# Last gate stage of a decoder layer: embedding products first, woven with the first gate tile

## The chip, the cores and the metric

The kernel runs on one core of a Trainium2 chip. Its time is that of one execution on the device, in microseconds (us). Three runs of the kernel before took 2184.57, 2187.47 and 2188.53 us; the median, 2187.47, is the time before.

## The reference

One layer of a decoder is computed for 1024 prompt positions and 8 single positions of other requests, together 1032 tokens (`N`), with 1024 channels. All of its stages lie ahead of the one that is changed, which is the end of the layer:

```python
    f = (jax.nn.silu(h2 @ w_ffn_gate) * (h2 @ w_ffn_up)) @ w_ffn_down
    x = x + rms_norm(f, ln_ffn_post)
    e = ple @ w_ple
    x = x + rms_norm(jax.nn.sigmoid(x @ w_ple_gate) * e, ln_ple_post)
```

`ple` is a per-layer input of 256 channels per token (`p_prompt`, `p_sample`), `w_ple` is 256 x 1024, `w_ple_gate` 1024 x 1024. The products `e` need `ple` alone; the gate needs the updated `x`.

## The kernel before, in words

The kernel is one program in stages, each with a barrier of all engines at its end. Within a stage every engine has its own list of instructions in the order in which the code issues them, and semaphores (`wait_ge`, `then_inc`) are all that sets the order between engines. Activations lie with channels on the 128 partitions and tokens along them: `X` is 8 chunks of 128 channels by 1032 tokens. A result tile is 128 output channels by 1032 tokens and takes three banks of PSUM (344 columns each); `acc` in PSUM has two such areas.

To keep fp32 accuracy at the speed of the faster matmul type, gate products are split: weights W = hi + lo (`WS`, parts 0 and 1), activations = hi + lo (`HH` and `XL`), and `split_tile` (L573) issues hi x HH, hi x XL, lo x HH, three matmuls each, for each of 8 chunks: 72 matmuls per tile. GpSimd splits the weights, with a cast (L581) and a subtraction (L583). The embedding products are plain fp32, in `gemm_tile` (L560): 2 chunks x 3 matmuls, each of which shows as two records.

The stage `ple` (L2370 on) does this:

- Entry. TensorE sums the squares of `f` per token (`row_sums`, L518); VectorE and ScalarE make the root's inverse (`RowRoot`, L546 to L553); TensorE spreads it over 128 partitions (`row_spread`, L526) into the second area of `acc`, called `flat`. SyncE has loaded the embedding input into `ptok`; TensorE transposes it (L2415, L2417) into `tp`, from where ScalarE copies it to `pT` (L2447).
- Update of X, chunk by chunk (c = 0 to 7): VectorE scales f by the gain and `flat` (L2467), adds it to X (L2470); ScalarE rounds X to `HH` (L2449); VectorE forms the remainder `XL` (L2473).
- Eight tiles m, as loops (`Fori`) on each engine. TensorE: 72 gate matmuls into area 0, then six embedding matmuls into area 1. ScalarE: sigmoid of area 0 to `SA` (L2453). VectorE: `SA` times area 1, into `F` chunk m (L2478). Then the square (ScalarE, L357), its sum (VectorE, L363) and the gain (ScalarE, L2457). Weights: SyncE loads the gate tile's into slot 0 of `W` and the embedding tile's into slot 1; GpSimd splits slot 0 into slot 0 of `WS` once `gate_done` says that TensorE is done with the tile before.

The first gate tile waits chunk by chunk for `XL` (`wait=(pe, x_lo)`). The stage after, `store_y`, adds the last norm and writes the output.

Of the kernel before, what the change touches and what calls it, by code (L numbers as in the profile page):

```python
# [508 lines left out]
def weight(ap, at, cols=P):  # L509

    return ap[:, bass.ds(at, cols)].rearrange("(c p) m -> p c m", p=P)
# [1858 lines left out]
def ple(k):  # L2370

    nc, g = k.nc, k.g
    with Stage(k, "ple") as st:
        acc = st.psum("acc", [P, 2, NT, 512])
        tp = st.psum("tp", [P, 2, 512])
        p_in, tr_done, tr_copied, gate_done, e_done, sig, gated, hi_done, split_done, slot_ok, spread, mixed, x_new, x_hi, x_lo, scaled = st.sems(
            "p_in tr_done tr_copied gate_done e_done sig gated hi_done split_done slot_ok spread mixed x_new x_hi x_lo scaled")
        ptok = k.E[:, 0:9 * 256].rearrange("p (t f) -> p t f", f=256)
        pT = chunks(k.Z[:, 8 * N:10 * N], 2)
        SA = k.E[:, 0:N]  # L2380
        squares = SquareSum(k, st)
        root = RowRoot(k, st, "post")
        flat = acc[:, 1].rearrange("p n w -> p (n w)")[:, 0:N]
        base = list(k.wcount)
        for s in range(2):
            k.wcount[s] += 8 * 16
        block = st.block()

        @block.sync
        def _(sp):  # L2390
            sp.dma_start(ptok[:, 0:TT, :], g["p_prompt"].rearrange("(t p) f -> p t f", p=P)).then_inc(p_in, 16)
            sp.dma_start(ptok[0:B, TT, :], g["p_sample"]).then_inc(p_in, 16)
            with sp.Fori(0, 8) as m:

                sp.wait_ge(split_done, m + 1)
                sp.dma_start(k.W[:, 0, 0:8, :], weight(g["w_ple_gate"], m * P)).then_inc(k.wfull[0], 16)
                sp.wait_ge(e_done, m + 1)
                sp.dma_start(k.W[:, 1, 0:2, :], weight(g["w_ple"], m * P)).then_inc(k.wfull[1], 16)

        @block.tensor  # L2400
        def _(pe):
            pe.sem_inc(gate_done, 1)
            pe.sem_inc(e_done, 1)
# [3 lines left out]
            pe.wait_ge(p_in, 32)  # L2407
            for c in range(2):
                for q in range(3):
                    n = 3 * c + q  # L2410
                    if n >= 2:
                        pe.wait_ge(tr_copied, n - 1)
                    if q < 2:
                        for t in range(4):
                            last = nc.tensor.transpose(tp[:, n % 2, t * P:(t + 1) * P], ptok[:, 4 * q + t, c * P:(c + 1) * P], k.ident[:])  # L2415
                    else:
                        last = nc.tensor.transpose(tp[:, n % 2, 0:B], ptok[0:B, TT, c * P:(c + 1) * P], k.ident[0:B, 0:B])  # L2417
                    last.then_inc(tr_done, 1)
            pe.wait_ge(tr_copied, 6)
            with pe.Fori(0, 8) as m:  # L2420
                pe.wait_ge(split_done, m + 2)
                pe.wait_ge(sig, m + 1)
                split_tile(k, acc, 0, 0, k.HH, k.XL, DC, wait=(pe, x_lo)).then_inc(gate_done, 1)
                pe.wait_ge(mixed, DC)
                pe.wait_ge(k.wfull[1], 16 * m + base[1] + 16)
                pe.wait_ge(gated, m + 1)
                gemm_tile(k, acc, 1, pT, 2).then_inc(e_done, 1)

        @block.gpsimd
        def _(pool):  # L2430
            pool.sem_inc(split_done, 1)
            with pool.Fori(0, 8) as m:
                pool.wait_ge(k.wfull[0], 16 * m + base[0] + 16)
                pool.wait_ge(gate_done, m + 1)
                pool.sem_inc(slot_ok, 1)
                split_weights(k, pool, 0, 0, DC, hi_done, m, split_done)

        @block.scalar
        def _(act):
            act.sem_inc(sig, 1)  # L2440
            root.scalar(act)
            for c in range(DC):
                if c < 6:
                    f, q = c // 3, c % 3
                    act.wait_ge(tr_done, c + 1)
                    a, w = (q * 512, 512) if q < 2 else (T, B)
                    nc.scalar.activation(pT[:, f, a:a + w], tp[:, c % 2, 0:w], ACT.Copy).then_inc(tr_copied, 1)  # L2447
                act.wait_ge(x_new, c + 1)
                nc.scalar.activation(k.HH[:, c, :], k.X[:, c, :], ACT.Copy).then_inc(x_hi, 1)  # L2449
            with act.Fori(0, 8) as m:  # L2450
                act.wait_ge(gate_done, m + 2)
                act.wait_ge(gated, m + 1)
                nc.scalar.activation(tokens(SA), acc[:, 0, :, 0:NW], ACT.Sigmoid).then_inc(sig, 1)  # L2453
                act.wait_ge(gated, m + 2)
                squares.square(act, one(k.F, m), m, 0)
                act.wait_ge(squares.squared, m + 1)
                nc.scalar.activation(one(k.F, m), one(k.F, m), ACT.Copy, scale=k.gains[:, 4, bass.ds(m, 1)]).then_inc(scaled, 1)  # L2457

        @block.vector
        def _(dve):  # L2460
            dve.sem_inc(gated, 1)
            root.clear(dve)
            root.vector(dve, acc[:, 0, 0, 0:9])
            dve.wait_ge(spread, 1)
            for c in range(DC + 1):
                if c < DC:
                    nc.vector.scalar_tensor_tensor(out=k.F[:, c, :], in0=k.F[:, c, :], scalar=k.gains[:, 3, c:c + 1], in1=flat,  # L2467
                                                   op0=ALU.mult, op1=ALU.mult).then_inc(mixed, 1)
# [6 lines left out]
            with dve.Fori(0, 8) as m:  # L2475
                dve.wait_ge(sig, m + 2)
                dve.wait_ge(e_done, m + 2)
                nc.vector.tensor_tensor(one(k.F, m), tokens(SA), acc[:, 1, :, 0:NW], ALU.mult).then_inc(gated, 1)  # L2478
                squares.add(dve, m, 0)
            dve.wait_ge(gated, 9)  # L2480
            dve.wait_ge(squares.summed, DC + 2)


# [144 lines left out]
```

## Time and profile before

| | us |
|---|---|
| runs | 2184.57, 2187.47, 2188.53; median 2187.47 |
| profiled execution, its own time | 2183.83 |
| its span, first to last instruction | 2182.1 |
| last gate stage, first matmul to end of its last sum | 1995.6 to 2151.9 |
| TensorE busy in the span | 2039.9 (93%) |
| VectorE, GpSimd, ScalarE busy | 754.3, 614.6, 507.6 |
| mean granted TensorE clock | 0.961 |

Over the whole span TensorE is the busy engine, but the change touches 7% of the span, so the shares of the whole say little here: read the stage's own stretches. Names of a tile in a row are those of its memory: `Z` holds `F`, `pT` and `XL`, `E` holds `ptok`, `SA` and the squares, `ple_acc` and `ple_tp` are the stage's PSUM. PE is TensorE's matmuls, PEld its weight loads, DVE VectorE, ACT ScalarE, POOL GpSimd, SPq the DMAs that SyncE issues.

### The profile page before, as it was taken

How to read it: one execution, taken by the hardware profiler on the slowest of the kernel's cores; microseconds unless marked ns; L12 is line 12 of the kernel's file. 1: busy time of each engine (PE TensorE's matmuls, PEld its weight loads, DVE VectorE, ACT ScalarE, POOL GpSimd, SP SyncE). 2: the span in 40 equal slices, each digit the busy share in tenths (PEclk: the TensorE clock that was granted, in tenths of full speed). 3: DMA queues.
4: the chain of work that ended last, by engine and by line, in shares of the span. 5: the costliest groups of instructions: out<-in, count | busy, mean ns of one | idle time of the engine just before them, and what ended most of it. 6: DMA issues, size and time to landing. Idle time of an engine off the chain costs nothing. (4 is left out here: it accounts for less than half of the span.)

```text
span 2182.1 us, 33339 instructions
## 1 busy us (share of the span) xinstructions
PE 2039.9 (93%) x13732; PEld 1944.9 (89%) x13732; DVE 754.3 (35%) x1440; ACT 507.6 (23%) x920; POOL 614.6 (28%) x506
## 2 busy tenths in 40 slices
PE   7999999976799989999989899999999999997897
PEld 6999989854688879999989899999999999996886
DVE  4104433233778863122231523012212322334413
ACT  5121011123577771010022311110000000012323
POOL 2323200001445553233332123232233323321110
PEclk9999999977899999999999799999999999998999
DMA  6233354133100011111122311111112112113012
GB/s 236 60 107 106 89 215 155 39 134 158 55 2 2 2 55 44 53 35 53 30 58 105 110 39 43 44 49 48 41 46 58 35 42 58 45 37 125 27 45 81
DMA packets 159027, 150.82 MB, mean 69 GB/s; under 512 B 18712, under 2 KB 151394, under 8 KB 156034
## 3 DMA queue, kind: packets, MB, share of 16 engines
q1 hardware_dynamic: 156082, 111.43, 16.7%
q0 software_dynamic: 2304, 33.56, 3.9%
q10 hardware_dynamic: 528, 4.23, 0.5%
q8 instruction: 83, 1.36, 0.3%
q14 instruction: 30, 0.25, 0.0%
HBM read 132.28 MB, written 21.10 MB: 70 GB/s over the span
## 5 line engine op out<-in xcount | busy, mean ns | idle before, releaser
L573 PE MATMUL ffn_acc<-HH,WS 128*128 128x344 f32 x2112 | 395.8, 322 | 8.4 <-DVE HL L505 7.3
L581 POOL CAST WS<-W 128x1024 fp32r<-128x1024 f32 (+2 forms) x125 | 130.9, 1047 | 901.2 <-PE ffn_acc L573 542.5
L573 PEld LDWEIGHTS ffn_acc<-HH,WS 128*128 128x128 f32 x2112 | 345.0, 189 | 8.8 <-issue 7.3
L583 POOL TENSOR_TENSOR WS<-W,WS 128x1024 fp32r<-128x1024 f32 (+2 forms) x125 | 294.7, 2357 | 10.0
L573 PE MATMUL ffn_acc<-HL,WS 128*128 128x344 f32 x1056 | 225.3, 322 | 0.0
L573 PE MATMUL ffn_acc<-AH,WS 128*128 128x344 f32 x1056 | 195.4, 320 | 0.0
L573 PEld LDWEIGHTS ffn_acc<-HL,WS 128*128 128x128 f32 x1056 | 179.9, 190 | 0.0
L573 PE MATMUL proj_acc<-HH,WS 128*128 128x344 f32 x912 | 174.4, 324 | 5.7 <-DVE HL L505 5.7
L573 PEld LDWEIGHTS ffn_acc<-AH,WS 128*128 128x128 f32 x1056 | 171.7, 188 | 0.0
L573 PEld LDWEIGHTS proj_acc<-HH,WS 128*128 128x128 f32 x912 | 149.0, 189 | 6.6 <-issue 4.1
L573 PE MATMUL merge_acc<-HH,WS 128*128 128x344 f32 x768 | 146.7, 323 | 7.0 <-DVE HL L505 7.0
L573 PEld LDWEIGHTS merge_acc<-HH,WS 128*128 128x128 f32 x768 | 126.8, 190 | 7.4 <-issue 5.6
L1029 PE MATMUL cmp_pre<-Hr,CW 128*128 128x254 f32 (+1 forms) x576 | 121.7, 371 | 2.7 <-DMA CW<-in_cmp_w_k 2.7
L1029 PEld LDWEIGHTS cmp_pre<-Hr,CW 128*128 128x128 f32 x576 | 105.0, 194 | 14.5 <-DMA CW<-in_cmp_w_k 2.9
L573 PE MATMUL ffn_acc<-AL,WS 128*128 128x344 f32 x528 | 111.7, 320 | 0.0
L1833 POOL TENSOR_SCALAR Hr<-Hr,tiny,gtok 128x128 f32<-128x128 f32 (+7 forms) x129 | 84.2, 661 | 93.4 <-DVE tiny L1913 63.3
L2343 DVE TENSOR_TENSOR E<-ffn_acc,R 128x1032 f32<-128x1032 f32 x22 | 27.1, 1233 | 221.9 <-PE ffn_acc L573 216.3
L2302 ACT ACTIVATE E<-E 128x1032 f32<-128x1032 f32 x22 | 23.5, 1068 | 334.8 <-DVE E L2343 334.8
L573 PE MATMUL proj_acc<-HL,WS 128*128 128x344 f32 x456 | 96.9, 321 | 0.0
L573 PEld LDWEIGHTS ffn_acc<-AL,WS 128*128 128x128 f32 x528 | 88.5, 188 | 0.0
L573 PE MATMUL ple_acc<-HH,WS 128*128 128x344 f32 x384 | 74.2, 325 | 10.2 <-ACT Z L2447 6.9
L573 PE MATMUL merge_acc<-HL,WS 128*128 128x344 f32 x384 | 82.3, 323 | 0.0
(408 smaller groups left out, 3325.5 us busy)
## 6 DMA issues: line engine op xcount, KB each, us to landing
W<-in_w_in SPq DMA_DIRECT2D x30, 512.0 KB, 3.9
W<-in_w_ffn_gate SPq DMA_DIRECT2D x22, 512.0 KB, 3.8
W<-in_w_ffn_up SPq DMA_DIRECT2D x22, 512.0 KB, 3.9
W<-in_w_ffn_down SPq DMA_DIRECT2D x16, 384.0 KB, 3.3
W<-in_w_ffn_down SPq DMA_DIRECT2D x16, 320.0 KB, 3.0
kept_x<-Z SPq DMA_DIRECT2D x1, 4128.0 KB, 13.4
Z<-kept_x SPq DMA_DIRECT2D x1, 4128.0 KB, 14.4
kept_x<-Z ACTq DMA_DIRECT2D x1, 4128.0 KB, 11.6
```

The lines of the kernel that those rows point to most:

```text
L573: last = k.nc.tensor.matmul(acc[:, s, n, 0:NW], k.WS[:, ws, part, c, :], src[:, c, n * NW:(n + 1) * NW], start=(c == 0 and part == 0 and s ...
L581: k.nc.gpsimd.tensor_copy(k.WS[:, ws, 0, 0:nk, :], w).then_inc(hi_done, 1)
L583: k.nc.gpsimd.tensor_tensor(k.WS[:, ws, 1, 0:nk, :], w, k.WS[:, ws, 0, 0:nk, :].bitcast(F32), ALU.subtract).then_inc(split_done, 1)
L1029: last = nc.tensor.matmul(pre[:, i, 0:2 * n].rearrange("p (g n) -> p g n", g=2), w1[:, i, c, :], TR[:, i, c % 8, :, c // 8:c // 8 + n], st ...
L1833: nc.gpsimd.tensor_scalar(x, x, li[s % 2][:, j:j + 1], k.gtok[:, t, 3 * h + r:3 * h + r + 1], ALU.mult, ALU.mult).then_inc(p_ready, 1)
L2302: nc.scalar.activation(SL, SL, ACT.Silu).then_inc(silu_done, 1)
L2343: nc.vector.tensor_tensor(tokens(SL), acc[:, 0, :, 0:NW], tokens(k.R1[:]), ALU.mult).then_inc(scaled, 1)
```

## The change

The stage is written straight out, without loops on the engines, and in another order.

- All of `w_ple` is loaded at once, into its own place `we`, ahead of the gate weights; these then take both slots of `W` and of `WS` in turn, and the first two loads wait for nothing.
- Eight of the transposes stand ahead of the row spread. The spread is copied to SBUF (`R1`) by ScalarE, and VectorE's scaling reads it there.
- The embedding product of chunk c goes into area 1 and is copied by ScalarE into `F` chunk c, whose old content has been used by then. On TensorE the products alternate with the chunks of gate tile 0: E0, E1, gate chunk 0, E2, gate chunk 1, and so on to gate chunk 7.
- Gate tiles 1 to 7 follow, in the two areas in turn. `SA` has two halves. VectorE multiplies `SA` by `F` chunk m, both in SBUF.

```diff
-            k.wcount[s] += 8 * 16
+            k.wcount[s] += 4 * 16
...
+            sp.dma_start(we, g["w_ple"].rearrange("(c p) m -> p c m", p=P)).then_inc(e_in, 16)
+            for m in range(8):
+                if m >= 2:
+                    sp.wait_ge(split_done, m - 1)
+                sp.dma_start(k.W[:, m % 2, 0:8, :], weight(g["w_ple_gate"], m * P)).then_inc(k.wfull[m % 2], 16)
...
             row_sums(k, acc[:, 0, 0, 0:9], k.ssq).then_inc(root.mean, 1)
+            pe.wait_ge(p_in, 32)
+            for n in range(2):
+                for t in range(4):
+                    last = nc.tensor.transpose(tp[:, n, t * P:(t + 1) * P], ptok[:, 4 * n + t, 0:P], k.ident[:])
+                last.then_inc(tr_done, 1)
             pe.wait_ge(root.rooted, 1)
             row_spread(k, flat, root.rs).then_inc(spread, 1)
...
-            with pe.Fori(0, 8) as m:
-                pe.wait_ge(split_done, m + 2)
-                pe.wait_ge(sig, m + 1)
-                split_tile(k, acc, 0, 0, k.HH, k.XL, DC, wait=(pe, x_lo)).then_inc(gate_done, 1)
-                pe.wait_ge(mixed, DC)
-                pe.wait_ge(k.wfull[1], 16 * m + base[1] + 16)
-                pe.wait_ge(gated, m + 1)
-                gemm_tile(k, acc, 1, pT, 2).then_inc(e_done, 1)
+            pe.wait_ge(r_copied, 1)
+            pe.wait_ge(e_in, 16)
+            for c in range(DC + 1):
+                if c < DC:
+                    if c:
+                        pe.wait_ge(e_copied, c)
+                    for i in range(2):
+                        for n in range(NT):
+                            last = nc.tensor.matmul(acc[:, 1, n, 0:NW], we[:, i, c * P:(c + 1) * P], pT[:, i, n * NW:(n + 1) * NW],
+                                                    start=(i == 0), stop=(i == 1))
+                    last.then_inc(e_done, 1)
+                if c:
+                    if c == 1:
+                        pe.wait_ge(split_done, 1)
+                        pe.wait_ge(root.inverse, 2)
+                    pe.wait_ge(x_lo, c)
+                    last = split_tile(k, acc, 0, 0, k.HH, k.XL, c, first=c - 1, more=c < DC)
+            last.then_inc(gate_done, 1)
+            for m in range(1, 8):
+                pe.wait_ge(split_done, m + 1)
+                if m == 1:
+                    pe.wait_ge(e_copied, DC)
+                else:
+                    pe.wait_ge(sig, m - 1)
+                split_tile(k, acc, m % 2, m % 2, k.HH, k.XL, DC).then_inc(gate_done, 1)
...
+            for m in range(8):
+                pool.wait_ge(k.wfull[m % 2], base[m % 2] + 16 * (m // 2 + 1))
+                if m >= 2:
+                    pool.wait_ge(gate_done, m - 1)
+                split_weights(k, pool, m % 2, m % 2, DC, hi_done, m, split_done)
...
             root.scalar(act)
+            turned(0)
+            turned(1)
+            act.wait_ge(spread, 1)
+            nc.scalar.activation(k.R1[:], flat, ACT.Copy).then_inc(r_copied, 1)
+            for n in range(2, 6):
+                turned(n)
             for c in range(DC):
                 act.wait_ge(x_new, c + 1)
                 nc.scalar.activation(k.HH[:, c, :], k.X[:, c, :], ACT.Copy).then_inc(x_hi, 1)
+                act.wait_ge(e_done, c + 1)
+                nc.scalar.activation(tokens(k.F[:, c, :]), acc[:, 1, :, 0:NW], ACT.Copy).then_inc(e_copied, 1)
+            for m in range(8):
+                act.wait_ge(gate_done, m + 1)
+                if m >= 2:
+                    act.wait_ge(gated, m - 1)
+                nc.scalar.activation(tokens(SA[:, m % 2, :]), acc[:, m % 2, :, 0:NW], ACT.Sigmoid).then_inc(sig, 1)
...
-            dve.wait_ge(spread, 1)
+            dve.wait_ge(r_copied, 1)
...
+                nc.vector.tensor_tensor(k.F[:, m, :], SA[:, m % 2, :], k.F[:, m, :], ALU.mult).then_inc(gated, 1)
```

On TensorE, at the stage's entry, behind the row sums (rows with - are of before, with + of after):

```order
 L518 MATMUL ple_acc<-ones,E 8x1
+L2406 MATMUL ple_tp<-ident,E 128x128 x8
 L526 MATMUL ple_acc<-ident,tiny 128x128 x8
 L526 MATMUL ple_acc<-ident,tiny 128x8
+L2418 MATMUL ple_tp<-ident,E 128x8
 L2415 MATMUL ple_tp<-ident,E 128x128 x8
-L2417 MATMUL ple_tp<-ident,E 128x8
-L2415 MATMUL ple_tp<-ident,E 128x128 x8
-L2417 MATMUL ple_tp<-ident,E 128x8
```

Half of the big transposes now stand ahead of the spread (L526).

On TensorE of before, the end of a tile in the loop:

```order
L573 MATMUL ple_acc<-XL,WS 128x344 x3
L573 MATMUL ple_acc<-HH,WS 128x344 x3
L2425 ISA
L560 MATMUL ple_acc<-Z,W 128x344 x6
L2420 REGISTER_ALU
L2420 COMPARE_AND_BRANCH
```

and of after, the beginning of the woven first tile (L2430 are the embedding products):

```order
L2430 MATMUL ple_acc<-Z 128x344 x12
L573 MATMUL ple_acc<-HH,WS 128x344 x3
L573 MATMUL ple_acc<-XL,WS 128x344 x3
L573 MATMUL ple_acc<-HH,WS 128x344 x3
L2430 MATMUL ple_acc<-Z 128x344 x6
```

The embedding products moved from behind each of the eight tiles to between the chunks of the first.

On ScalarE, what stands between the entry and the second chunk of X (HH is the rounded X, the last row the copy of an embedding product):

```order
+L2463 ACTIVATE Z<-ple_tp 128x512 x2
+L2469 ACTIVATE R<-ple_acc 128x1032
+L2463 ACTIVATE Z<-ple_tp 128x8
+L2463 ACTIVATE Z<-ple_tp 128x512 x2
+L2463 ACTIVATE Z<-ple_tp 128x8
+L2474 ACTIVATE HH<-X 128x1032
+L2476 ACTIVATE Z<-ple_acc 128x1032
```

All six copies of the transposed input now stand ahead of the first HH, and a product's copy behind each HH.

## Rows read from the trace of the kernel before

**Rows 1.** Busy us by stretch: length, PE, PEld, DVE, ACT, POOL (x instructions), clock, DMA, GB/s.
```profile
2004.50:2022.60 18.10, 4.16 (x18) 2.97 (x19) 17.91 (x15) 7.50 (x11) 2.09 (x1) 0.59 0.10 29
...
2039.90:2147.90 108.00, 105.30 (x588) 94.72 (x588) 17.15 (x14) 31.79 (x28) 20.33 (x12) 1.00 0.13 38
```
**Rows 2.** Timeline of one tile: start, duration, engine, line, instruction, idle before.
```profile
2039.96 0.46 PEld L573 LDWEIGHTS ple_acc<-HH,WS 128*128 128x128 f32 x3 [0.93 <-issue]
...
2051.24 3.24 PEld L560 LDWEIGHTS ple_acc<-Z,W 128*128 128x128 f32 x12
2051.39 3.63 PE L560 MATMUL ple_acc<-Z,W 128*128 128x344 f32 x12
...
2051.73 1.04 POOL L581 CAST WS<-W 128x1024 fp32r<-128x1024 f32 x1 [11.98 <-PE ple_acc L573]
2052.84 2.35 POOL L583 TENSOR_TENSOR WS<-W,WS 128x1024 fp32r<-128x1024 f32 x1
...
2055.44 0.71 PE L573 MATMUL ple_acc<-HH,WS 128*128 128x344 f32 x3 [0.41 <-POOL WS L583]
```
**Rows 3.** Timeline of the stage's entry and of the update of X.
```profile
1995.29 0.39 SPq L2391 DMA_DIRECT2D E<-in_p_prompt  x1
...
1995.63 3.67 PE L518 MATMUL ple_acc<-ones,E 128*128 128x1 f32 x18 [5.08 <-PEq L90]
...
2000.18 4.30 PE L526 MATMUL ple_acc<-ident,tiny 128*128 128x128 f32 x18 [0.88 <-ACT tiny L553]
...
2004.52 1.29 DVE L2467 SCALAR_TENSOR_TENSOR Z<-Z,gains,ple_acc 128x1032 f32<-128x1032 f32 x1 [4.64 <-PE ple_acc L526]
2005.54 0.60 ACT L2447 ACTIVATE Z<-ple_tp 128x512 f32<-128x512 f32 x1 [5.41 <-PE ple_tp L2415]
2005.85 1.83 DVE L2470 TENSOR_TENSOR X<-X,Z 128x1032 f32<-128x1032 f32 x1
...
2009.31 1.12 PE L2415 MATMUL ple_tp<-ident,E 128*128 128x128 f32 x4 [2.90 <-ACT Z L2447]
...
2022.60 1.20 PE L573 MATMUL ple_acc<-HH,WS 128*128 128x344 f32 x3 [6.95 <-ACT Z L2447]
...
2029.27 1.28 DVE L2467 SCALAR_TENSOR_TENSOR Z<-Z,gains,ple_acc 128x1032 f32<-128x1032 f32 x1
```
**Rows 4.** Short stretches of the entry and of the first tile (columns of rows 1).
```profile
1996.50:2000.00 3.50, 2.80 (x15) 2.69 (x15) 0.43 (x3) 0.23 (x2) 0.00 (x0) 0.50 0.90 292
...
2022.60:2025.80 3.20, 3.20 (x11) 3.20 (x12) 3.17 (x4) 1.07 (x1) 0.00 (x0) 0.50 0.00 0
...
2005.00:2005.50 0.50, 0.50 (x5) 0.50 (x4) 0.50 (x1) 0.00 (x0) 0.50 (x1) 0.66 0.00 0
```
**Rows 5.** The gate weights' loads: issue to landing.
```profile
DMA to landing us min/median/max: 3.9/4.0/6.3
```
**Rows 6.** Timeline of the projection stage: gate-type (L573) and fp32 (L754) matmuls.
```profile
244.20 0.64 PE L573 MATMUL proj_acc<-HH,WS 128*128 128x344 f32 x3
244.68 3.73 PE L754 MATMUL proj_acc<-Z,E 128*128 128x128 f32 x32
248.17 0.71 PE L573 MATMUL proj_acc<-HH,WS 128*128 128x344 f32 x3
```
**Rows 7.** Timeline of the stage's end.
```profile
2143.74 0.64 PE L573 MATMUL ple_acc<-HH,WS 128*128 128x344 f32 x3
...
2144.48 1.28 ACT L2453 ACT_TABLE_LOAD   x1 [8.08 <-PE ple_acc L573]
2145.78 1.03 ACT L2453 ACTIVATE E<-ple_acc 128x1032 f32<-128x1032 f32 x1
2148.08 1.23 DVE L2478 TENSOR_TENSOR Z<-E,ple_acc 128x1032 f32 x1 [11.71 <-PE ple_acc L560]
...
2150.63 1.23 DVE L363 TENSOR_TENSOR E<-E 128x1032 f32<-128x1032 f32 x1 [1.33 <-ACT E L357]
```
**Rows 8.** The same add in the stage before: duration ns min/median/max.
```profile
L2331 DVE TENSOR_TENSOR Z<-Z x8: 1232/1232/2420, 1205.3 to 1233.6; 128x1032 f32<-128x1032 f32 x8
```

More of the change, by code:

```diff
@@ L2405, in _ @@
             pe.wait_ge(root.rooted, 1)
             row_spread(k, flat, root.rs).then_inc(spread, 1)
[L2407 to L2418, printed above, removed]
@@ L2419, in _ @@
-            pe.wait_ge(tr_copied, 6)
-            with pe.Fori(0, 8) as m:
-                pe.wait_ge(split_done, m + 2)
-                pe.wait_ge(sig, m + 1)
-                split_tile(k, acc, 0, 0, k.HH, k.XL, DC, wait=(pe, x_lo)).then_inc(gate_done, 1)
-                pe.wait_ge(mixed, DC)
-                pe.wait_ge(k.wfull[1], 16 * m + base[1] + 16)
-                pe.wait_ge(gated, m + 1)
-                gemm_tile(k, acc, 1, pT, 2).then_inc(e_done, 1)
+            for n in range(2, 6):
+                q = n % 3
+                pe.wait_ge(tr_copied, n - 1)
+                if q < 2:
+                    for t in range(4):
+                        last = nc.tensor.transpose(tp[:, n % 2, t * P:(t + 1) * P], ptok[:, 4 * q + t, P:2 * P], k.ident[:])
+                else:
+                    c = n // 3
+                    last = nc.tensor.transpose(tp[:, n % 2, 0:B], ptok[0:B, TT, c * P:(c + 1) * P], k.ident[0:B, 0:B])
+                last.then_inc(tr_done, 1)
@@ L2438, in _, with turned @@
         @block.scalar
         def _(act):
-            act.sem_inc(sig, 1)
-            root.scalar(act)
-            for c in range(DC):
[L2443 to L2447, printed above, removed]
+            def turned(n):
+                f, q = n // 3, n % 3
+                act.wait_ge(tr_done, n + 1)
+                a, w = (q * 512, 512) if q < 2 else (T, B)
+                nc.scalar.activation(pT[:, f, a:a + w], tp[:, n % 2, 0:w], ACT.Copy).then_inc(tr_copied, 1)
@@ L2448, in _ @@
+            root.scalar(act)
+            turned(0)
+            turned(1)
+            act.wait_ge(spread, 1)
+            nc.scalar.activation(k.R1[:], flat, ACT.Copy).then_inc(r_copied, 1)
+            for n in range(2, 6):
+                turned(n)
+            for c in range(DC):
                 act.wait_ge(x_new, c + 1)
                 nc.scalar.activation(k.HH[:, c, :], k.X[:, c, :], ACT.Copy).then_inc(x_hi, 1)
-            with act.Fori(0, 8) as m:
-                act.wait_ge(gate_done, m + 2)
+                act.wait_ge(e_done, c + 1)
+                nc.scalar.activation(tokens(k.F[:, c, :]), acc[:, 1, :, 0:NW], ACT.Copy).then_inc(e_copied, 1)
@@ L2465, in _ @@
             for c in range(DC + 1):
                 if c < DC:
[L2467 removed]
+                    nc.vector.scalar_tensor_tensor(out=k.F[:, c, :], in0=k.F[:, c, :], scalar=k.gains[:, 3, c:c + 1], in1=k.R1[:],
                                                    op0=ALU.mult, op1=ALU.mult).then_inc(mixed, 1)
@@ L2474, in _ @@
             squares.start(dve)
[L2475 to L2480, printed above, removed]
+            dve.wait_ge(e_copied, DC)
+            for m in range(8):
+                dve.wait_ge(sig, m + 1)
+                nc.vector.tensor_tensor(k.F[:, m, :], SA[:, m % 2, :], k.F[:, m, :], ALU.mult).then_inc(gated, 1)
+                squares.add(dve, m, m % 2)
+            dve.wait_ge(gated, 8)
             dve.wait_ge(squares.summed, DC + 2)
```

29 lines of the change are left out of this document (8 added, 21 removed).

## The prediction

> **What bounds the kernel now.** Read the stretches first: which engine works through the last gate stage, and when. From 2004.50 to 2022.60 us TensorE is busy 4.16 of 18.10 us, while VectorE updates X chunk by chunk; in the seven tiles after the first one TensorE is busy 105.30 of 108.00 us [rows 1]. So the stage has a part in which TensorE stands still and a part in which nothing else matters. The timeline of one tile gives the price of each: weight loads of the gate products begin at 2039.96 and those of the embedding products at 2051.24, so 72 gate matmuls take 11.28 us; six embedding products take 3.63 us; then TensorE waits 0.41 us for GpSimd, which can split the next weights only when the gate tile is over, since there is one buffer [rows 2]. A tile takes 108.00/7 = 15.43 us [rows 1]. ScalarE and VectorE are off this path except at the end [rows 7].
>
> The timeline of the entry shows why TensorE stands still [rows 3]: row sums end at 1999.30, the row spread runs 2000.18 to 2004.48, VectorE starts its eight chunks at 2004.52, and the transposes of the embedding input wait for ScalarE, whose copies stand between the HH copies. The gate tile begins at 2022.60 after a wait of 6.95 us on the last of those copies. Nothing in the embedding products needs X: this idle time can take them.
>
> **The change, part by part.** I place everything on the profile's clock and compare the end of the stage, 2150.63 + 1.23 = 2151.86 us before [rows 7]. What follows it (norm, transposes, stores) is unchanged and is counted at nothing.
>
> *Entry, later than before.* Eight transposes now stand between the row sums and the spread, and wait for the embedding input. It is issued at 1995.29 [rows 3] and has 1.05 MB (sizes here are the shapes' elements, four bytes each); at 292 GB/s [rows 4] from 1996.5 its bytes are there at 2000.1, and I add 0.8 (an estimate) until its semaphore is up: 2000.9. At the low clock four transposes took 1.12 us [rows 3], eight 2.2, so the spread starts at 2003.1 instead of 2000.18 and ends after 4.30 at 2007.4. Bounds: 1999.3, where TensorE is ready anyway, so 1.6 earlier; and the case that the queue mixes its transfers (rival A). VectorE now waits for ScalarE's copy of the spread to SBUF as well, 0.1 + 1.03 (the sigmoid of the same shape [rows 7]): its chain starts at 2008.5, 4.0 later. That is covered, below.
>
> *First embedding product.* After the spread: its copy 1.13, four transposes 1.12, their copy 0.10 + 0.60 [rows 3], and 0.6 (an estimate) for the 8-column pieces and hand-overs: 3.5, hence 2010.9. Its weights, 1 MB behind the embedding input, are due 1.05/0.292 = 3.6 us after it, near 2004.5; the first two gate tiles' weights 1.8 us each behind, 2006.3 and 2008.1, and their splits of 3.5 us (2051.73 to 2055.19 [rows 2]) end near 2009.8 and 2013.3. All before they are needed.
>
> *TensorE's work.* The sum of products is what it was: 8 x (11.28 + 3.63) = 119.3 us. Added waits:
> - The second product wants the area of the first, with no gate chunk between: 0.1 + 1.03 for ScalarE's copy, 1.2 in all.
> - From the third on a gate chunk, 9 x 11.28/72 = 1.41 us, stands between, against 0.1 + 1.03 + 0.05 = 1.18 for the copy: hidden. The cover is thin, so 0.5 for six, with bounds of nothing and 0.5 each.
> - Clock. The first tile of before ran 2022.60 to 2025.80 at 0.50 (1.2 GHz), then at 2.4 GHz. It had been at 2.4 GHz already from about 2005.3 on, when the spread and eight transposes had run one behind the other, and was lost again in the idle time [rows 4]. Now spread, transposes and products follow each other with gaps of about 1 us, so the first product may start at either level: nothing or 1.6 (half of 3.2); I take 0.8.
> - Waits of gate chunks for X: XL of chunk 0 is due 8 us into VectorE's chain (two rounds of 3.54, the first and last of eight starts being 2004.52 and 2029.27 [rows 3], and hand-overs), near 2016, with two splits beside it 2018.4 at worst; the chunk is wanted after the second product, at 2010.9 + 0.8 + 3.63 + 1.2 + 3.63 = 2020.2. Later, VectorE needs 3.54 per chunk and TensorE 3.63 + 1.41 = 5.04. No wait; should the cover go, it costs at most the 1 to 2 us by which XL would be late.
> - Going to and fro between the two kinds of product: in the projection, also written straight out, gate-type matmuls end at 244.84, fp32 ones start at 244.68 and the next gate-type start at 248.17 before those end at 248.41 [rows 6]. Nothing, from both sides; the same rows price straight-line code.
>
> So the last gate product ends at 2010.9 + 119.3 + 1.2 + 0.5 + 0.8 = 2132.7.
>
> *Tiles 1 to 7.* Two weight slots and two accumulators: the split (3.5 us) now lies under an 11.28 us tile, and the 0.41 wait [rows 2] goes, seven times. A sigmoid must have read an accumulator two tiles later: 11 us of cover. Next late would be ScalarE, 31.79/7 = 4.5 us busy per tile [rows 1]: far off.
>
> *Tail.* Before, the last embedding product hid the sigmoid; now sigmoid 0.10 + 1.03, then multiply, square, sum, 2151.86 - 2148.08 = 3.78 [rows 7]: with 0.05 hand-over 4.95. The table load (1.28) happens once, at the first tile, not on the path. End: 2137.7. Against 2151.86 that is 14.2 us less. The multiply now reads two SBUF operands; nothing splits weights beside the last one.
>
> Profiled execution: 2183.83 - 14.2 = 2169.6 us. It lies 3.64 below the median 2187.47 of the runs; by the median the forecast is **2173.3 us**.
>
> **Two rules weighed.** VectorE's add took 1.83 instead of 1.23 with a split beside it [rows 3], and the same kind in the stage before up to 2.42 [rows 8]. The Trainium skill (SBUF — State Buffer, "SBUF: two separate sides") says that VectorE with two SBUF inputs and GpSimd take a shared port pair by exclusive lock, and the loser stands for the whole instruction; the trace agrees. It speaks against this change, since the scaled add now takes the spread from SBUF: two splits at worst 2.4 us on VectorE's chain. By the rule the end moves only if the 1.8 to 4 us of cover named above fail.
>
> The gate weights, issued behind the embedding input, landed after 6.3 us [rows 5]. The skill (DMA: Bandwidth & Descriptors, "Queues, rings and completion order") says that each DMA engine consumes descriptors in ring order; by it the megabyte of weights now queued behind does not delay the input. No row has the input's own landing.
>
> **Rivals.**
> - A, the transfers share the queue: the embedding input lands with the last of 1.05 + 1.05 + 0.52 + 0.52 = 3.14 MB, 10.8 us after 1996.5 at 292 GB/s, at 2007.3 instead of 2000.9. Everything in the stage moves by up to 6.4: 2176 to 2179.7. For it: nothing waited on this transfer, so its landing is unseen. Against: the gate weights behind it landed within 6.3 us [rows 5], in which 292 GB/s move 1.8 MB, hardly more than these two transfers (1.57).
> - B, hand-overs: each product waits half a microsecond for its area, and a lock delays the first gate chunk: 7 x 0.5 - 0.5 + 1.5 = 4.5: 2177.8. For it: a cover of 1.41 against 1.18. Against: ScalarE starts 0.10 after a tile's end [rows 7].
> - C, the slower one: the clock. If TensorE's waits in the woven first tile keep it at 1.2 GHz, its 8 x 3.63 + 11.28 = 40.3 us take 40.3 longer: 2213. It decides from 14.2 us of work at half clock. For it: the clock stood at 0.50 at the start of the first tile. Against: it rose 3.2 us after that start, although that tile had waits too.
> - D, straight-line code: some 580 matmuls that were a loop of 78 must be fetched. 1.25 us lost per tile eats 10 us: 2183, no change. Against: the projection's straight tiles run without a gap [rows 6].
>
> **Chances and range.** Forecast 0.62, A 0.15, B 0.15, D 0.05, C 0.03. Best: input there at once (-1.6), no waits (-0.5), warm start (-0.8), and the medians' scatter of 2 to 3 us: about 2166. Worst of A and B together reaches 2184; 2182 leaves out that corner, C and most of D. Range 2166 to 2182. Faster by over 0.2% (4.4 us, about what can be told from no change): forecast, A and B, 0.92; same, D, 0.05; slower, C, 0.03.
>
> **What would show it.** First embedding product near 2011, last gate product near 2133, tiles 1 to 7 at 11.3 us with no wait on GpSimd, woven chunks at 5.0 us, one table load for eight sigmoids, transposes starting near 2001, stage end near 2138. Wrong if chunks take over 5.6, if VectorE's XL is named before a gate chunk, or if the granted clock is 0.5 after the first product.

## The result, and the profile after

The changed kernel takes 2169.32 us (median of four runs, 2163.83 to 2171.33), the kernel before 2186.78 beside it (four runs, 2184.57 to 2188.53): a ratio of 0.9912, with a 95% interval of 0.9893 to 0.9931. The forecast was 2173.3 and "faster". The profiled execution's own time is 2169.65.

Because the part of the program ahead of the stage takes a few microseconds more or less from one execution to the next, I compare lengths inside one profile: from the start of the row sums (L518) to the end of the last sum (L363). Before, this was 2151.86 - 1995.63 = 156.23 us [rows 3, 7]; after, 140.23. Measured from the issue of the embedding input it is 156.57 and 140.28: 16.3 us less, of a forecast 14.2.

The stretches first, with the columns of [rows 1]: the end of the entry, the first embedding product, the woven tile, tiles 1 to 7.

```profile
2006.80:2010.40 3.60, 2.55 (x18) 1.92 (x17) 1.40 (x1) 2.21 (x5) 3.45 (x3) 0.97 0.33 81
2010.50:2013.50 3.00, 3.00 (x5) 1.84 (x6) 2.96 (x3) 0.06 (x1) 2.92 (x2) 0.50 0.56 168
2014.00:2052.80 38.80, 37.68 (x164) 28.40 (x163) 29.00 (x23) 16.82 (x17) 1.62 (x1) 1.00 0.05 14
2052.90:2132.50 79.60, 79.59 (x505) 79.30 (x503) 22.54 (x14) 22.84 (x21) 26.39 (x12) 1.00 0.09 27
```

The 14 us in which TensorE stood still while VectorE updated X [rows 1] are gone: from 2014 on it is idle 1.1 us in all, and in the seven tiles not at all. What is new is the second line: right after a stretch at 0.97 the first product starts at 0.50, that is 1.2 GHz.

The timeline of the entry (start, duration, engine, line, instruction, idle before and what ended it):

```profile
1997.01 0.39 SPq L2392 DMA_DIRECT2D E<-in_p_prompt  x1
...
1997.06 3.67 PE L518 MATMUL ple_acc<-ones,E 128*128 128x1 f32 x18 [4.78 <-PEq L90]
...
2002.60 1.97 PE L2406 MATMUL ple_tp<-ident,E 128*128 128x128 f32 x8 [1.88 <-DMA E<-in_p_sample]
...
2004.36 3.54 PE L526 MATMUL ple_acc<-ident,tiny 128*128 128x128 f32 x18
...
2009.08 0.66 PE L2415 MATMUL ple_tp<-ident,E 128*128 128x128 f32 x4 [0.54 <-ACT Z L2463]
...
2010.49 5.38 PE L2430 MATMUL ple_acc<-Z 128*128 128x344 f32 x12 [0.60 <-ACT Z L2463]
...
2013.33 3.38 DVE L2495 SCALAR_TENSOR_TENSOR Z<-Z,gains,R 128x1032 f32<-128x1032 f32 x1
...
2017.00 3.74 PE L2430 MATMUL ple_acc<-Z 128*128 128x344 f32 x12 [1.12 <-ACT Z L2476]
2017.90 1.23 DVE L2501 TENSOR_TENSOR XL<-X,HH 128x1032 fp32r<-128x1032 f32 x1
...
2020.31 0.90 PE L573 MATMUL ple_acc<-HH,WS 128*128 128x344 f32 x3
```

The transposes wait 1.88 us for the input, the second product 1.12 for its area. VectorE's second scaling takes 3.38 instead of 1.29 [rows 3], with a weight split beside it; still the first XL is ready at 2019.13, before the first gate chunk wants it at 2020.31, which shows no wait.

Two of the woven chunks, and the end (same columns):

```profile
2040.33 1.03 ACT L2476 ACTIVATE Z<-ple_acc 128x1032 f32<-128x1032 f32 x1 [2.90 <-PE ple_acc L2430]
...
2041.56 3.63 PE L2430 MATMUL ple_acc<-Z 128*128 128x344 f32 x12
...
2045.22 1.03 ACT L2476 ACTIVATE Z<-ple_acc 128x1032 f32<-128x1032 f32 x1 [2.91 <-PE ple_acc L2430]
```

```profile
2131.85 0.64 PE L573 MATMUL ple_acc<-HH,WS 128*128 128x344 f32 x3
2132.53 1.03 ACT L2481 ACTIVATE E<-ple_acc 128x1032 f32<-128x1032 f32 x1 [6.67 <-PE ple_acc L573]
2133.59 1.23 DVE L2506 TENSOR_TENSOR Z<-E,Z 128x1032 f32<-128x1032 f32 x1 [7.66 <-ACT E L2481]
...
2136.06 1.23 DVE L363 TENSOR_TENSOR E<-E 128x1032 f32<-128x1032 f32 x1 [1.24 <-ACT E L357]
```

A woven chunk takes 4.89 us, with no wait ahead of the product. The end, from the last matmul to the last sum, is 2137.29 - 2132.49 = 4.80 us.

### The profile page after: what moved, and what is told of

It is laid out like the page before. It is cut to its first block and busy times, and to the rows that moved or that the text cites. A ratio compares the mean times of both kernels' runs of the same rounds, so it can differ in the third digit from the quotient of the medians.

```text
span 2167.8 us, 33107 instructions
## 1 busy us (share of the span) xinstructions
PE 2041.6 (94%) x13732; PEld 1949.5 (90%) x13732; DVE 762.9 (35%) x1440; ACT 507.4 (23%) x922; POOL 621.9 (29%) x506
## 3 DMA queue, kind: packets, MB, share of 16 engines
q8 instruction: 87, 1.43, 0.3%
## 5 line engine op out<-in xcount | busy, mean ns | idle before, releaser
L573 PE MATMUL ffn_acc<-HH,WS 128*128 128x344 f32 x2112 | 395.7, 322 | 8.5 <-DVE HL L505 7.4
L573 PEld LDWEIGHTS ffn_acc<-HH,WS 128*128 128x128 f32 x2112 | 345.0, 189 | 8.9 <-issue 7.5
L583 POOL TENSOR_TENSOR WS<-W,WS 128x1024 fp32r<-128x1024 f32 (+2 forms) x125 | 301.6, 2413 | 10.0
L573 PE MATMUL ffn_acc<-HL,WS 128*128 128x344 f32 x1056 | 225.2, 322 | 0.0
L573 PE MATMUL ffn_acc<-AH,WS 128*128 128x344 f32 x1056 | 195.4, 320 | 0.0
L573 PE MATMUL proj_acc<-HH,WS 128*128 128x344 f32 x912 | 174.3, 324 | 7.3 <-DVE HL L505 7.3
L573 PEld LDWEIGHTS ffn_acc<-HL,WS 128*128 128x128 f32 x1056 | 179.8, 190 | 0.0
L573 PEld LDWEIGHTS ffn_acc<-AH,WS 128*128 128x128 f32 x1056 | 171.7, 188 | 0.0
L573 PEld LDWEIGHTS proj_acc<-HH,WS 128*128 128x128 f32 x912 | 149.1, 189 | 8.0 <-issue 6.0
L573 PE MATMUL merge_acc<-HH,WS 128*128 128x344 f32 x768 | 146.8, 323 | 6.8 <-DVE HL L505 6.8
L573 PEld LDWEIGHTS merge_acc<-HH,WS 128*128 128x128 f32 x768 | 126.9, 191 | 7.3 <-issue 5.5
L573 PE MATMUL ffn_acc<-AL,WS 128*128 128x344 f32 x528 | 111.7, 319 | 0.0
L573 PE MATMUL proj_acc<-HL,WS 128*128 128x344 f32 x456 | 97.2, 322 | 0.0
L573 PEld LDWEIGHTS ffn_acc<-AL,WS 128*128 128x128 f32 x528 | 88.5, 188 | 0.0
L573 PE MATMUL merge_acc<-HL,WS 128*128 128x344 f32 x384 | 82.3, 323 | 0.0
L2350 DVE TENSOR_TENSOR E<-E,ffn_acc 128x1032 f32<-128x1032 f32 x22 | 27.1, 1230 | 151.8 <-PE ffn_acc L573 151.8
```

Of the source, the lines that this page charges most:

```text
L573: last = k.nc.tensor.matmul(acc[:, s, n, 0:NW], k.WS[:, ws, part, c, :], src[:, c, n * NW:(n + 1) * NW], start=(c == 0 and part == 0 and s ...
L583: k.nc.gpsimd.tensor_tensor(k.WS[:, ws, 1, 0:nk, :], w, k.WS[:, ws, 0, 0:nk, :].bitcast(F32), ALU.subtract).then_inc(split_done, 1)
L2350: nc.vector.tensor_tensor(tokens(GU), tokens(SL), acc[:, 1, :, 0:NW], ALU.mult).then_inc(gated, 1)
```

## The experiments

All lengths below run from the start of the row sums to the end of the last sum; a length in an "expected" text that is counted from the issue of the input is 0.05 us more (before the change 0.34). Before: 156.23; changed kernel, "after" below: 140.23, 140.38 and 140.41 in three profiles. The table sums up what each kernel's profile shows.

| kernel | stage, us | first product starts after, lasts | second product's wait |
|---|---|---|---|
| before | 156.23 | - | - |
| two slots only | 154.65 | - | - |
| changed, one weight slot | 186.85 | 13.40, 3.74 | 1.12 |
| changed, not woven | 147.16 | 13.39, 3.74 | 1.42 |
| changed, spread first | 138.79 | 13.10, 3.74 | 1.12 |
| changed | 140.23 | 13.43, 5.38 | 1.12 |
| two areas | 139.09 | 13.69, slow | none |
| weights issued first | 143.27 | 16.49, 5.43 | 1.12 |
| input early (two profiles) | 136.03 | 10.77, 3.74 | 1.12 |
| all early, two areas (two profiles) | 133.35 | 9.36 and 9.41, fast | none |

**Two weight slots in the order of before.** The stage of before, written straight out, with `w_ple` loaded at once and both slots; its order of work kept:

```diff
-                sp.wait_ge(split_done, m + 1)
-                sp.dma_start(k.W[:, 0, 0:8, :], weight(g["w_ple_gate"], m * P)).then_inc(k.wfull[0], 16)
+                if m >= 2:
+                    sp.wait_ge(split_done, m - 1)
+                sp.dma_start(k.W[:, m % 2, 0:8, :], weight(g["w_ple_gate"], m * P)).then_inc(k.wfull[m % 2], 16)
```

> The order of before (embedding product behind each gate tile), but w_ple loaded at once and two slots for the gate weights; written straight out like after. The stage's length, from the issue of the embedding input to the end of its last sum, was 156.6 us before and 140.3 after. Theory (the gain is idle time of TensorE at the entry that the products fill): only the 0.41 us waits go and seven loop ends with them, 3 us: stage 153 to 154, some 2183 us. Rival (the gain is the second slot and the straight code): stage near 141, some 2170 us.

Measured: 2183.21 us (ten runs), a ratio of 0.9992 (0.9983 to 1.0002); stage 154.65, near the theory's 153 to 154 and far from the rival's 141. The tiles' period fell from 15.43 to 14.84 us, 7 x 0.59 = 4.1 us; but the first gate tile begins 2.7 us later (2026.14 - 1996.50 = 29.64 behind the start of the row sums, before 2022.60 - 1995.63 = 26.97), and the timeline shows why:

```profile
2008.99 2.35 POOL L583 TENSOR_TENSOR WS<-W,WS 128x1024 fp32r<-128x1024 f32 x1
2009.19 3.24 DVE L2474 TENSOR_TENSOR X<-X,Z 128x1032 f32<-128x1032 f32 x1
...
2013.40 3.21 POOL L583 TENSOR_TENSOR WS<-W,WS 128x1024 fp32r<-128x1024 f32 x1
...
2014.33 1.28 DVE L2471 SCALAR_TENSOR_TENSOR Z<-Z,gains,ple_acc 128x1032 f32<-128x1032 f32 x1
2015.64 2.07 DVE L2474 TENSOR_TENSOR X<-X,Z 128x1032 f32<-128x1032 f32 x1
...
2026.14 1.23 PE L573 MATMUL ple_acc<-HH,WS 128*128 128x344 f32 x3 [6.53 <-ACT Z L2450]
```

The second split now also falls into the update of X, and there VectorE's chain is on the path. The add with both inputs in SBUF stands until GpSimd's subtraction ends (2011.34) and finishes 1.09 later, while the scaling that reads the spread from PSUM keeps its 1.28. So of 16 us the slots and the straight code alone give 1.6, and no time that these runs tell from none; the rest comes only with the new order.

**One weight slot in the order of after.** One slot in `W` and one in `WS`:

```diff
-                if m >= 2:
-                    sp.wait_ge(split_done, m - 1)
-                sp.dma_start(k.W[:, m % 2, 0:8, :], weight(g["w_ple_gate"], m * P)).then_inc(k.wfull[m % 2], 16)
+                if m >= 1:
+                    sp.wait_ge(split_done, m)
+                sp.dma_start(k.W[:, 0, 0:8, :], weight(g["w_ple_gate"], m * P)).then_inc(k.wfull[0], 16)
```

> After, but with one slot for the gate weights: the split of a tile's weights starts when the tile before is done. Theory: the embedding products had covered this split, and nothing covers it now: 0.1 + 3.5 + 0.2 us per tile, seven times, 26 to 30 us: stage 167 to 171, slower than before (2195 to 2200 us). Rival (the split lies beside other work anyway): stage 140 to 143.

Measured: 2216.08 us, ratio 1.0141 (1.0124 to 1.0158); stage 186.85, 46.6 us longer than after. The direction was expected, the size not: the expected text has waits of 3.8 us and nothing for the clock. The waits of TensorE's gate matmuls in tiles 1 to 7, and two stretches of one tile (columns of [rows 1]), a wait and what follows it:

```profile
  POOL WS L583: 32.2, 7
```

```profile
2068.80:2073.40 4.60, 0.03 (x1) 0.03 (x1) 2.28 (x2) 3.14 (x3) 4.32 (x2) 1.00 0.00 0
2073.40:2077.00 3.60, 3.60 (x14) 3.60 (x15) 1.01 (x1) 0.11 (x1) 0.00 (x0) 0.58 0.50 145
```

Seven waits of 4.6 us are 32.2 (the subtraction takes 3.29 there, since VectorE's multiply has started beside it); the rest, 46.6 - 32.2 and 1.6 more because the first product ran fast here, is 16 us or 2.3 per tile, which fits the second stretch: for 3.6 us after the wait the granted clock is 0.58, so most of these matmuls ran at 1.2 GHz. So the second slot, worth at most 4.1 us in the tiles of the old order, where the embedding product covered the split, is worth 46.6 in the new one: order and slots are one change.

**Not woven: all products first, in one area.**

```diff
-            for c in range(DC + 1):
-                if c < DC:
+            for c in range(DC):
...
-                    last = split_tile(k, acc, 0, 0, k.HH, k.XL, c, first=c - 1, more=c < DC)
+            split_tile(k, acc, 0, 0, k.HH, k.XL, DC, wait=(pe, x_lo)).then_inc(gate_done, 1)
```

> After, but all eight embedding products stand ahead of gate tile 0, in one area: each waits for the copy of the one before (0.1 + 1.03 + 0.05 us) with no gate chunk between. Theory (the weave hides six copies): 6 x 1.1 to 1.2 us more, stage 147, some 2176 us. Rival (order of these is all one, TensorE is late at the X chunks anyway): stage 140 to 141.

Measured: 2176.57 us (one run); stage 147.16, as expected. Each product waits for ScalarE's copy of the one before:

```profile
2020.50 3.74 PE L2428 MATMUL ple_acc<-Z 128*128 128x344 f32 x12 [1.12 <-ACT Z L2469]
...
2025.35 3.74 PE L2428 MATMUL ple_acc<-Z 128*128 128x344 f32 x12 [1.12 <-ACT Z L2469]
```

The pitch is 4.85 instead of 3.47 us; 1.38 x 6 = 8.3, less 1.64 for a first product that ran fast here. The weaving hides six of the seven copies.

**Spread first again.**

```diff
+            pe.wait_ge(root.rooted, 1)
+            row_spread(k, flat, root.rs).then_inc(spread, 1)
             pe.wait_ge(p_in, 32)
             for n in range(2):
...
-            pe.wait_ge(root.rooted, 1)
-            row_spread(k, flat, root.rs).then_inc(spread, 1)
```

> After, but the row spread stands ahead of the eight transposes again, as before, and the copy of the spread ahead of those of the transposes. Theory (the first product waits for the transposes' copies either way): spread ends 1 to 2 us earlier, first product within 0.7 us of the 13.5 us after the issue of the embedding input that it had; stage 140 to 141. Rival (the late landing of the input, 5.6 us after its issue, costs the whole entry): stage 137 to 138.

Measured: 2168.85 us (one run); stage 138.79, between the 140 to 141 that I expected and the rival's 137 to 138.

```profile
2002.27 4.30 PE L526 MATMUL ple_acc<-ident,tiny 128*128 128x128 f32 x18 [0.88 <-ACT tiny L553]
...
2010.82 3.74 PE L2430 MATMUL ple_acc<-Z 128*128 128x344 f32 x12 [0.34 <-ACT Z L2463]
...
2016.16 3.39 DVE L2499 TENSOR_TENSOR XL<-X,HH 128x1032 fp32r<-128x1032 f32 x1
...
2019.70 0.71 PE L573 MATMUL ple_acc<-HH,WS 128*128 128x344 f32 x3 [0.29 <-DVE XL L2499]
```

The first product starts 0.33 us earlier, as the theory said, and runs at 2.4 GHz, which gives another 1.64. Together that is 1.97, but the stage is only 1.44 shorter: the other half a microsecond is lost by the first gate chunk, which here waits for XL, whose subtraction took 3.39 us instead of 1.23 beside the second weight split. Moving eight transposes ahead of the spread gained nothing here.

**Two areas for the first three products.**

```diff
+        def area(c):
+            return 1 if c >= 3 else (3 - c) % 2
...
-                    if c:
-                        pe.wait_ge(e_copied, c)
+                if c >= 2:
+                    pe.wait_ge(e_copied, c - 1 if c < AHEAD else c)
```

> The changed kernel with three embedding products ahead of the first gate chunk, which alternate between both accumulator areas (first in area 1, second in area 0, third and all later ones in area 1), so that the second product needs no copy of the first; nothing is left out. Lengths are from the issue of the embedding input to the end of the stage's last sum; the changed kernel has 140.28 us, 138.84 with the spread first and a warm first product. Theory (the second product's wait for its area is 1.1 us and lies on the path, the clock of the first product decides another 1.6): the second product starts 3.5 us after a warm first one or 5.1 after a slow one, with no wait on ScalarE; stage 139.2 with a slow first product, 137.5 with a warm one; tiles 1 to 7 at 11.37. Rival (the wait only moves: ScalarE's copies or the X chain come late at the first gate chunk instead): stage 140 to 141, with a wait of about 1 us ahead of the first gate chunk.

Measured: stage 139.09, 1.14 less than after, as expected with a slow first product. Three products run without a wait, and the first gate chunk follows at once:

```profile
2017.62 12.35 PE L2438 MATMUL ple_acc<-Z 128*128 128x344 f32 x36 [0.60 <-ACT Z L2476]
...
2029.54 0.90 PE L573 MATMUL ple_acc<-HH,WS 128*128 128x344 f32 x3
```

Its time, 2170.91 us (2168.97 to 2175.33), shows no gain over the changed kernel beside it (next): 1.1 us is less than the scatter.

**The changed kernel again**, for the clock of the first product and for the scatter.

> The changed kernel itself once more, unchanged, to have it beside the two others on one chip. Every theory: 2167 to 2171 us, stage 139 to 140.5 us from the issue of the embedding input. What is asked is the first embedding product: by the theory that the clock at its start hangs on details of the gap ahead of it and not on the code, it may run at either level, 3.7 or 5.4 us; by the rival that the changed kernel's order sets it, it takes 5.4 again.

> The changed kernel a third time, beside the one with the unloaded entry. Every theory: 2167 to 2171 us, stage 140.2 to 140.5 us with a slow first product (5.4 us), 138.7 with a fast one (3.7), feed-forward stage beginning at 1195 to 1198.

Measured: 2167.86 and 2166.73 us, ratios 0.9925 (0.9912 to 0.9939) and 0.9908 (0.9895 to 0.9922); the first product took 5.41 and 5.39. The feed-forward stage began at 1195.70 and 1200.46 us (1195 to 1198 had been expected for the second): 4.8 us of scatter that lie ahead of the change.

**Input early.** The embedding input alone is loaded during the feed-forward stage (its last rows into another tile):

```diff
+            sp.wait_ge(a_lo, sum(FFN_PARTS) + 1)
+            sp.dma_start(k.E[:, 0:TT * 256].rearrange("p (t f) -> p t f", f=256), g["p_prompt"].rearrange("(t p) f -> p t f", p=P)).then_inc(k.ple_p, 16)
+            sp.dma_start(k.sel[0:B, 0:256], g["p_sample"]).then_inc(k.ple_p, 16)
```

> The changed kernel with one thing altered: the embedding input alone is loaded during the feed-forward stage, so that the transposes ahead of the spread wait for no DMA; nothing is left out. Lengths from the first matmul of the row sums: 140.23, 140.38 and 140.41 us in three profiles of the changed kernel. In all traces so far with that entry the first product ran at 1.2 GHz at first (5.4 us) where the wait for the input was 1.88 to 2.08 us (four), and at 2.4 GHz (3.7 us) where it was 1.85 or 1.87 (two). Theory (the wait itself, 1.9, goes, and with less idle time ahead of it the first product is fast, another 1.6): transposes 3.6 us after the entry, first product near 11.7 instead of 13.4 and in 3.7 us, second product still waiting 1.1, stage 136.6 to 137.2. Rival (the slow first product has nothing to do with that wait): first product as early, in 5.4, stage 138.4 to 138.8.

> The kernel with the embedding input alone loaded early, once more and unchanged. Its stage was 136.03 us in its profile, 4.4 less than the changed kernel's 140.4, yet its median of 2167.82 us lay beside the changed kernel's 2166.7 to 2169.3. In the profiled execution the feed-forward stage began at 1202.30 us; in three executions of the changed kernel it began at 1197.46, 1195.70 and 1200.46. Theory (scatter of the part ahead, as among those three): stage 135.9 to 136.2 again with a fast first product, the feed-forward stage beginning at 1195 to 1201, and a median of 2162 to 2166. Rival (this kernel's code itself makes the part ahead of the feed-forward stage longer): it begins at 1201 or later again and the median stays at 2167 to 2169.

Measured: stage 136.03 in both profiles, 4.2 to 4.4 less, and 0.6 better than the theory.

```profile
2005.39 1.97 PE L2408 MATMUL ple_tp<-ident,E 128*128 128x128 f32 x8
...
2007.15 2.81 PE L527 MATMUL ple_acc<-ident,tiny 128*128 128x128 f32 x18
...
2012.57 3.74 PE L2432 MATMUL ple_acc<-Z 128*128 128x344 f32 x12 [0.60 <-ACT Z L2465]
```

Entered at 2001.80, the first product starts at 10.77 instead of 13.43 and lasts 3.74 instead of 5.38: 2.66 + 1.64 = 4.3. Of the 2.66, 1.95 are the wait and 0.73 come from the spread, which takes 2.81 instead of 3.54. Times: 2167.82, then 2165.11 us; the mean of the eight runs, 2166.6, lies 1.9 below that of the changed kernel's fourteen (2168.5), which these runs hardly tell from nothing, and less than the stage's 4.3. Where the rest went is open; the feed-forward stage was not longer (799.50 and 799.56 us to the row sums, 799.60 in after). In the first profile the feed-forward stage began at 1202.30, in the second at 1196.92, so the rival of the second text (the altered code lengthens the part before) falls.

**Weights issued first.** Two lines of SyncE's list exchanged:

```diff
+            sp.dma_start(we, g["w_ple"].rearrange("(c p) m -> p c m", p=P)).then_inc(e_in, 16)
             sp.dma_start(ptok[:, 0:TT, :], g["p_prompt"].rearrange("(t p) f -> p t f", p=P)).then_inc(p_in, 16)
...
-            sp.dma_start(we, g["w_ple"].rearrange("(c p) m -> p c m", p=P)).then_inc(e_in, 16)
```

> The changed kernel with two lines of SyncE's list exchanged: the embedding weights (1.05 MB) are issued ahead of the embedding input instead of behind it; nothing is left out. Theory (transfers of one queue land in the order of their issue, so the megabyte ahead delays the input by its own 3.6 us): the transposes wait 5 to 6 us instead of 1.9, the first product is at 16.5 to 17.5 us behind the first issue instead of 13.5, stage 143 to 145. Rival A of the prediction (the transfers share the queue and land together, whichever is issued first): the wait changes by less than 1 us, stage 140 to 141.

Measured: 2175.77 us (one run); stage 143.27.

```profile
1999.95 0.39 SPq L2392 DMA_DIRECT2D Z<-in_w_ple  x1
...
2008.18 1.97 PE L2406 MATMUL ple_tp<-ident,E 128*128 128x128 f32 x8 [4.52 <-DMA E<-in_p_sample]
...
2016.48 5.43 PE L2430 MATMUL ple_acc<-Z 128*128 128x344 f32 x12 [0.60 <-ACT Z L2463]
```

The transposes start 8.23 us behind the first issue instead of 5.59: 1.05 MB ahead costs 2.64 us, less than the expected 3.6, and what 1.05 MB take at 1.05/2.64 = 400 GB/s. The order of issue counts: a megabyte ahead of the input costs what its bytes take. That the weights behind the input don't delay it in the changed kernel follows from this but has no run of its own. The Trainium skill (DMA: Bandwidth & Descriptors, "Queues, rings and completion order") says that each DMA engine consumes its descriptors in ring order; the trace agrees, with this 2.64.

**All early, two areas.** Input, embedding weights and two gate tiles' weights during the feed-forward stage; all transposes ahead of the spread, in four banks; four products ahead of the first gate chunk, in both areas in turn:

```diff
+            for s in range(2):
+                sp.wait_ge(split_done, 2 * sum(FFN_PARTS) + 8 * len(parts) + 1 + s)
+                sp.dma_start(k.W[:, s, 0:8, :], weight(g["w_ple_gate"], s * P)).then_inc(k.wfull[s], 16)
...
+        pieces = [(0, 0, tp[:, 0, :]), (0, 1, tp[:, 1, :]), (1, 0, acc[:, 0, 1, :]), (1, 1, acc[:, 0, 2, :]),
+                  (0, 2, acc[:, 0, 0, 16:16 + B]), (1, 2, acc[:, 0, 0, 32:32 + B])]
```

> The changed kernel with its entry unloaded: the embedding input, the embedding weights and the first two gate tiles' weights are loaded during the feed-forward stage before, into places that are free by then; the transposes follow the row sums with no wait for a DMA and in four PSUM banks, and stand ahead of the spread whole; four embedding products stand ahead of the first gate chunk in both areas in turn. Nothing is left out. No DMA marks the entry, so lengths are from the first matmul of the row sums to the end of the last sum: 156.23 us before the change, 140.23 in the changed kernel. Theory (of the changed kernel's entry some 1.9 us are the wait for the input and 1.1 the second product's wait for its area; the splits of the first two tiles delay VectorE's X only beside it): no wait on a DMA, first product about 11.5 us after the entry instead of 13.4, second product without a wait, stage 135.6 to 137.2, time 2164 to 2166. Rival (the entry is bound by something else, ScalarE's copies or VectorE's chain, or the moved transfers cost the stage before as much): stage 139 to 141 or the stage before longer by 2 to 4, time 2168 to 2171.

> The kernel with the unloaded entry once more, unchanged. In its first profile the stage took 133.35 us from the first row sum (140.38 in the changed kernel beside it), 7.0 less, but its median was only 4.0 us less, and in the profiled execution the feed-forward stage began 5.0 us later than beside it (1200.68 against 1195.70), ahead of everything that was altered. Theory (that delay is scatter between executions of an unchanged part): the stage takes 133 to 134 again, the feed-forward stage is 799.4 to 799.8 long again and begins anywhere from 1195 to 1201, and the mean of all runs of both labels lies 4 to 7 us below the changed kernel. Rival (the altered kernel itself delays the part before): it begins at 1200 to 1201 again, and the gain in time stays 2 to 4.

Measured: 2163.89 and 2163.35 us, ratios to before 0.9895 (0.9880 to 0.9910) and 0.9889 (0.9874 to 0.9904); stage 133.35 both times, better than expected.

```profile
2000.15 3.67 PE L520 MATMUL ple_acc<-ones,E 128*128 128x1 f32 x18 [4.77 <-PEq L90]
...
2003.75 1.97 PE L2420 MATMUL ple_tp<-ident,E 128*128 128x128 f32 x8
...
2007.22 2.36 PE L528 MATMUL ple_acc<-ident,tiny 128*128 128x128 f32 x18
...
2009.51 2.00 PE L2440 MATMUL ple_acc<-Z,R 128*128 128x344 f32 x6
2011.35 1.90 PE L2440 MATMUL ple_acc<-Z 128*128 128x344 f32 x6
```

From the row sums on TensorE has no wait ahead of the products. The first starts 4.07 us earlier than in after, is not slow (1.64), and the second doesn't wait (1.12): 6.8 of the 6.9 us. This version beats both kernels: the mean of its eight runs is 2163.4 us. The 5.1 us to the changed kernel's 2168.5 are less than the stage's 6.9. The feed-forward stage was not longer in its first profile (799.47 us to the row sums, 799.60 in after) and was 802.26 in the second, where 799.4 to 799.8 had been expected; it began at 1200.68 and 1197.36. The moved loads didn't lengthen it: the difference is there when SyncE issues the third gate weights' load of that stage, 54.84 us after its start instead of 52.05, and the first moved load is issued more than 700 us later (1970.20). Four to eight runs can't say whether the missing 2 us are scatter.

## Why the prediction was right, step by step

Times are counted from the issue of the embedding input (1995.29 before, 1997.01 after).

| step | predicted | measured |
|---|---|---|
| transposes start, input there | 5.61 | 5.59 |
| spread ends | 12.1 | 10.89 |
| first embedding product starts | 15.6 | 13.48 |
| clock of the first product costs | 0.8 | 1.64 |
| wait of the second product | 1.2 | 1.12 |
| six hand-overs | 0.5 | 0 |
| a tile of 72 gate matmuls | 11.28 | 11.37 |
| an embedding product | 3.63 | 3.47 |
| first product to last gate product's end | 121.8 | 122.0 |
| tail | 4.95 | 4.80 |

- The mechanism held at each step: the idle time was taken by the products, the 0.41 us per tile went, one table load served all sigmoids (at 2051.17), VectorE's longer chain was covered.
- The term that was mis-sized is the entry, 2.1 us too long, and it is the whole difference between 16.3 and 14.2. More than half of it is the clock: I priced the spread and the four transposes behind it at the low clock of [rows 3]. In the changed kernel transposes and spread follow each other without a gap, and the clock rose during the spread: it took 3.54 instead of 4.30, and four transposes 0.66 instead of 1.12, together 1.22. The other 0.9 is no clock. The eight transposes ahead of the spread did run at 0.50, yet the spread began 1.76 us after them and not 2.2, because I had added up the lengths of records, which overlap; and of the 0.6 that I allowed for the 8-column pieces and hand-overs about 0.1 was needed. The earlier profile had shown the rise near 2005.3 [rows 4]; I used it for the product's start and not for what ran before.
- The first product's clock was left open between nothing and 1.6; it cost 1.64. The six hand-overs were overpriced, since the cover of 1.41 against 1.18 was enough. That the stretch from the first product on came out within 0.2 us of the forecast is partly luck: 0.84 more for the clock stands against 0.5 less for the hand-overs and the next point's 0.07 per tile.
- An embedding product's record lasts 3.63, but the next begins 3.47 after it: the kernel with two slots shows the sum, a tile period of 14.84 = 11.37 + 3.47. The error of the two terms together is 0.07 per tile.
- Rival A (transfers share the queue) fell: the input came at 5.59, and the exchange of two lines shows what a megabyte ahead would cost. B (hand-overs) fell by the trace. C (the clock) did not happen after the first product, but the kernel with one slot shows that its price is real: 2.3 us after each wait of 4.6. D (straight-line code) fell: 79.59 of 79.60 us busy.
- The rule of the exclusive lock (the Trainium skill, SBUF — State Buffer, "SBUF: two separate sides") applied: 3.38 us for a scaling and 1.95 for an add. It stayed off the path here, with 1.2 us left of the cover (XL ready at 2019.13, wanted at 2020.31). It was on the path in the kernel with two slots only, where the first gate tile came 2.7 us later, and in the one with the spread first, where the first gate chunk waited for XL: the cover is thin. By it whoever starts first keeps the ports; the trace agrees from the other side too, as in tiles 1 to 7 the split starts just behind VectorE's multiply and takes (count, then minimum, median and maximum in ns)

```profile
L583 POOL TENSOR_TENSOR WS<-W,WS x6: 3343/3348/3415, 2054.2 to 2111.0; 128x1024 fp32r<-128x1024 f32 x6
```

  against 2.35 before [rows 2], which costs nothing under an 11.37 us tile.

The time itself was 4.0 us below the forecast: 2.1 from the entry, and 0.7 because the median of before came out at 2186.78 beside it and not at 2187.47; the last 1.2 is less than the difference between executions. That the profiled execution took 2169.65 us where the working had 2169.6 is luck: the stage gained 2.1 us more, but its row sums began 1.43 us later than before (1997.06 against 1995.63), and 0.27 was lost behind the stage.

## What to carry to other kernels

Look for the stretch in which the busiest engine waits for another one's chain, and for work on it that needs none of that chain's results; then count what the moved work used to hide, for here the embedding products had covered the weight splits, and without a second slot the new order was 30 us slower than the old one. Price the instructions around the idle time at both levels of the clock, because filling the gap changes the level of what was there. When the stage begins with a load that depends on nothing in it, load it a stage earlier: 4.2 to 4.4 of the next 7 us in the stage came from one transfer, though the time of the whole program showed only 1.9 of them.

## What was not expected

- The clock of the first product. With the same instructions ahead of it, it ran fast in two kernels, whose transposes had waited 1.85 and 1.87 us for the input, and slow in four profiles with 1.88, 1.96, 2.08 and 2.08 us; with 4.52 slow, with no wait fast (four profiles). That the wait bears on it is shown by the kernel with the input early: without the wait the product was fast in both profiles, though the time from the end of the spread to the product was the same (2012.57 - 2009.96 = 2.61 us, 2010.49 - 2007.90 = 2.59 in after). The longer wait changed nothing. Two waits 0.01 apart that end differently are an observation and no rule, and what sets the clock there stays open.
- Executions of one program differ by several us ahead of the change (the feed-forward stage began between 1195.70 and 1200.46 us in three), so 1 us in the stage can be seen in a profile and not in four runs.
- The transfers of the entry moved faster than I had read. While the first transposes ran, the weights behind the input came at 390 GB/s, against 292 in [rows 4]; but that 292 is a mean over a stretch that holds the start of the transfers, and the kernel before moved 387 GB/s between 1998 and 1999 too.

```profile
2002.60:2004.30 1.70, 1.70 (x8) 1.70 (x9) 0.00 (x0) 0.55 (x1) 0.00 (x0) 0.50 0.99 390
```
